# A decoder layer on one core: another queue order for the last two gated units, and three means in a row

## The chip, the cores and the metric

The kernel runs on one core of a Trainium2 chip. TensorE (PE) multiplies matrices into PSUM banks; PEld is its loading of weights. VectorE (DVE), ScalarE (ACT) and GpSimd (POOL) work beside it, each with an instruction row of its own; the SyncE queue (SP) issues nearly all DMAs. Engines wait for one another by semaphores only. The metric is the device time of one execution in microseconds (us), the median of several. TensorE's clock has two levels, 2.4 and 1.2 GHz; the profile shows which one was granted, 1.00 being the higher.

## The reference, cut to what matters

One layer of a decoder (DEPTH is 1) over 1024 prompt rows and 8 sample rows, 1032 columns in all. In the first half a combined projection feeds two groups of heads:

```
proj = x @ w_in            # q, f, i, g: 4 heads x 128 (HGRN2), u: 32 groups x 16 (S5)
f = lb + (1 - lb) * sigmoid(fz); k = (1 - lb) * sigmoid(-fz)
o_A: S_t = diag(f_t) S_{t-1} + k_t v_t^T, o_t = S_t^T q_t       # per head
o_A = o_A * rsqrt(mean(o_A^2) + eps) * norm_g * sigmoid(g)      # per head
o_B = gelu(C h + D u); o_B = o_B * sigmoid(o_B @ w_glu)         # S5
x = LayerNorm(alpha * x + concat(o_A, o_B) @ w_out)
x = LayerNorm(alpha * x + ConvFFN(x))
```

The means over 128 channels of the squares of a head's output, the sigmoid of g and the glu product with its sigmoid are what the change moves. ConvFFN is the second half and isn't touched.

## The kernel before

Data lies transposed: channels on the 128 partitions, the 1032 columns in the free dimension, in three blocks of 344. Products are made in three passes from high and low halves (wh and XH hold rounded values, wl and XL what is left), so every weight and activation that TensorE uses is first split: the high half by a copy on ScalarE, the low half by a subtraction on VectorE.

The first half is a list of steps, written by `order()` and walked by every engine. Each engine emits its own part of a step, so the list sets the order of instructions on all of them:

- `part n i` is product i of unit n on TensorE: one block of 128 rows, 3 passes x 3 column blocks, 9 matmuls of 344 columns. Units 0 to 3 are u, 4 to 15 are f, q, g of heads 0 to 3 (so 14 is q and 15 is g of head 3, the two of `DIRECT`, which stay on the chip), 16 to 19 the glu product, 20 and 21 the first two blocks of the out projection. Even units use slot 0 of weights and banks, odd ones slot 1.
- `unit n` follows the last product of a unit: ScalarE evacuates its banks (a sigmoid for 15 to 19) and makes the high half of the weights of unit n + 2.
- `lo n` is the low half of the weights of unit n on VectorE. `with_splits` puts it in: it becomes due at `unit n-2` and is written behind the second following step of the kinds part, level, values, kt, kv, o.
- `level h l` (0 to 7) is the within-chunk work of head h. TensorE does small matmuls into one of two banks, VectorE reads the bank and extends QK, from level 6 on ScalarE copies. TensorE's level l needs VectorE's step of level l - 1.
- `kt`, `kv`, `o`: transposed keys, chunk states, and the output products of a head. With `o` ScalarE copies the output and squares it. `ms h b` is the mean of block b: a matmul with a matrix of 1/128 on TensorE, Ln and Exp on ScalarE. `fin h b` multiplies output, factor and gate on VectorE. `hp_sig` and `hp_a` prepare a head.
- `gelu`, `gl`: high and low halves of the gelu rows. `z m`, `zh m`, `zl m`: glu gate row m on VectorE, its high half on ScalarE, its low half on VectorE.

Steps that are not products stand in tables, `S5_SLOTS`, `SLOTS` (one row for each head, one string for each level) and `TAIL`. A digit in a string takes as many products from a queue. The queue is filled with units in their order and, at two points, with parts of units. `put` holds the last product of unit 14 back until `("o", 1)` is in the list, and that of unit 15 until `("fin", 1, 2)` is. In a row of `SLOTS` a head's own levels stand with the `kt` to `fin` steps of the head before.

`level`, `kt`, `kv`, `o`, `ms` share two banks in turn; `bank_uses` numbers them in the order of the list. TensorE waits until the last use of the bank has been read. Ln and Exp lie in one table of ScalarE, the sigmoid in another; a table is loaded (L1060, L1133, L1163) wherever the kind changes.

Of the kernel before, what the change touches and what calls it, by code (L numbers as in the profile page):

```python
# [23 lines left out]
KD = D // P  # L24
# [59 lines left out]
DIRECT = (14, 15)  # L84


def rows_of(n):

    if n < GLU_N:
        return list(range(KD))  # L90
    if n < OUT_N:
        return list(range(HEADS))
    return list(range(HEADS, KD)) + list(range(HEADS))
# [21 lines left out]
]  # L115
TAIL = "kt 1 kv 2 o save rload wh2 wl2 2 ms0 1 ms1 1 f30 m30 ms2 1 f31 l30 m31 f32 ahead p30 l31 m32 wh3 l32 p31 p32"

def order():


    o, queue = [], []

    def unit(n, parts=None):

        last = len(rows_of(n)) - 1
        return [(1.32, [("part", n, i)] + ([("unit", n)] if i == last else []) +
                 ([(Z_AFTER[i], n - 1 - GLU_N)] if GLU_N < n < OUT_N and i in Z_AFTER else []))
                for i in (range(last + 1) if parts is None else parts)]
# [92 lines left out]
    o.append(("wv", 0))  # L221
    for n in (2, 3, *range(F_N, DIRECT[0])):
        queue += unit(n)
    queue += unit(14, range(4)) + unit(15, range(4)) + unit(14, range(4, KD)) + unit(15, range(4, KD))
    values = iter([NC, *range(NC)])
    for c in range(HEADS):
        for step, slot in zip(S5_STEPS, S5_SLOTS[c]):
# [42 lines left out]


ORDER = order()


# [2639 lines left out]
```

## Time and profile before

| | us |
|---|---|
| median of 3 runs | 1202.02 (1201.29 to 1203.36) |
| the profiled execution | 1200.96 |
| its span, first to last instruction | 1199.2 |
| TensorE busy | 1169.8 (98%) |
| VectorE busy | 814.6 (68%) |
| ScalarE busy | 507.8 (42%) |
| GpSimd busy | 181.1 (15%) |

The mean granted clock of TensorE is 0.997. Lines as L1657 are those of the kernel: L1657 is `part`, L1646 and L1676 the out projection, L1805 to L1827 the levels, L1836 `kt`, L1843 `kv`, L1854, L1855 and L1860 `o`, L1866 `ms`; on VectorE L2389 extends QK, L2423 is `kv`, L2437 and L2443 are `fin`, L2450 is `lo`, L2516 and L2517 are `z`, L2218 makes low halves; on ScalarE L1201 to L1206 are `o`, L1215 and L1217 `ms`, L1126 and L1133 units, L1068 high halves of weights, L1141 `zh`, L1222 `gelu`. The stretch that the change touches lies between 292 and 400 us.

The page has busy time of each engine, a strip of 40 slices, the DMA queues, the chain of work that ended last, and groups of instructions. A timeline lists instructions in order of time with the idle time before them in brackets and what ended it. "issue" is time in which the engine waited for nothing that the profile shows.

### The profile page before, as it was taken

What the parts mean: (1) busy time and instruction counts of PE and PEld (TensorE: products, weight loads), DVE (VectorE), ACT (ScalarE), POOL (GpSimd) and SP (SyncE); (2) the same over time, 40 slices, a digit from 0 to 9 for tenths busy, and PEclk for the clock granted to TensorE, in tenths of its full rate; (3) what the DMA queues carried; (4) which work ended last, traced back from release to release, by engine and by line L of the source; (5) the groups of instructions that cost most, each with busy time, mean ns of one, the idle gap of its engine ahead of it and who ended that gap; (6) DMA issues with size and microseconds to landing.
All of it is one profiled execution on the core that took longest, in us unless ns stands there. A gap on an engine that the chain in (4) does not pass through costs nothing.

```text
span 1199.2 us, 24092 instructions
## 1 busy us (share of the span) xinstructions
PE 1169.8 (98%) x9718; PEld 1129.0 (94%) x9718; DVE 814.6 (68%) x1498; ACT 507.8 (42%) x850; POOL 181.1 (15%) x152
## 2 busy tenths in 40 slices
PE   9999999999898999999999999999999999999996
PEld 8988889998788999999999999999999999999995
DVE  6995767557887557798627863686458844786547
ACT  5411212337756446665314541354125521554335
POOL 5210000100000244200210021001200030001365
PEclk9999999999999999999999999999999999999999
DMA  8441223518435410411372227222631255112503
GB/s 301 117 119 50 89 78 122 179 58 220 123 105 183 178 36 37 142 37 46 89 258 90 55 64 273 98 65 55 227 146 55 56 181 191 55 56 60 206 25 119
DMA packets 84815, 139.31 MB, mean 116 GB/s; under 512 B 26360, under 2 KB 52504, under 8 KB 84696
## 3 DMA queue, kind: packets, MB, share of 16 engines
q1 hardware_dynamic: 84704, 137.77, 35.9%
q8 instruction: 78, 1.28, 0.4%
q14 instruction: 33, 0.27, 0.1%
HBM read 97.89 MB, written 40.03 MB: 115 GB/s over the span
## 4 chain that ended last, share of the span: by engine, by line
PE 84%; DVE 10%; ACT 2%; issue 2%; DMA 1%; POOL 0%; SPq 0%; POOLq 0%; ACTq 0%; DVEq 0%
PE psum L1973 32%; PE psum L1945 15%; PE psum L1657 13%; PE psum L1676 6%; PE psum L2056 5%; PE psum L1734 4%; PE psum L1646 1%; DMA st<-in_xT 1%; DVE R L2583 1%; PE psum L1787 1%; PE psum L1769 1%; DVE wl L2631 1%; PE psum L1782 1%; PE psum L1854 1%; PE psum L1816 1%
## 5 line engine op out<-in xcount | busy, mean ns | idle before, releaser
L1973 PE MATMUL psum<-XH,wh 128*128 128x258 f32 x640 | 181.3, 283 | 1.7 <-ACT ub L1324 1.4
L1973 PE MATMUL psum<-XH,wl 128*128 128x258 f32 x640 | 181.0, 283 | 0.0
L1973 PE MATMUL psum<-TR,wh 128*128 128x258 f32 x640 | 181.0, 283 | 0.0
L1973 PE MATMUL psum<-XL,wh 128*128 128x258 f32 x640 | 180.0, 282 | 0.0
L1587 POOL TENSOR_TENSOR wl<-raw,wh 128x512 fp32r<-128x512 f32 (+2 forms) x36 | 57.8, 1610 | 567.8 <-ACT wh L1273 557.1
L1945 PE MATMUL psum<-AH,wl 128*128 128x344 f32 x384 | 123.1, 321 | 0.0
L1973 PEld LDWEIGHTS psum<-XH,wh 128*128 128x128 f32 x640 | 121.0, 189 | 2.2 <-issue 2.2
L1945 PE MATMUL psum<-AL,wh 128*128 128x344 f32 x384 | 123.1, 320 | 0.0
L1945 PE MATMUL psum<-AH,wh 128*128 128x344 f32 x384 | 122.9, 320 | 0.0
L1973 PEld LDWEIGHTS psum<-XL,wh 128*128 128x128 f32 x640 | 121.5, 190 | 0.1
L1973 PEld LDWEIGHTS psum<-XH,wl 128*128 128x128 f32 x640 | 120.9, 189 | 0.0
L1973 PEld LDWEIGHTS psum<-TR,wh 128*128 128x128 f32 x640 | 120.9, 189 | 0.0
L1657 PE MATMUL psum<-XH,wh 128*128 128x344 f32 x477 | 110.3, 340 | 2.0 <-DVE wl L2450 1.1
L1324 ACT ACTIVATE ub<-psum 128x258 f32<-128x258 f32 x160 | 58.8, 380 | 109.1 <-DVE hb L2649 60.1
L1657 PE MATMUL psum<-XL,wh 128*128 128x344 f32 x477 | 101.6, 321 | 0.8 <-DVE XL L2218 0.8
L1657 PE MATMUL psum<-XH,wl 128*128 128x344 f32 x477 | 101.3, 321 | 0.0
L1273 ACT ACTIVATE wh<-WS 128x512 fp32r<-128x512 f32 x80 | 50.5, 631 | 114.2 <-DVE WS L2624 114.1
L1273 ACT ACTIVATE wh<-raw 128x512 fp32r<-128x512 f32 (+2 forms) x96 | 61.2, 639 | 86.5 <-PE psum L1945 44.9
L1973 PE MATMUL psum<-TH,wh 128*128 128x258 f32 x320 | 90.8, 284 | 1.8 <-DVE wl L2631 1.5
L1973 PE MATMUL psum<-TH,wl 128*128 128x258 f32 x320 | 90.2, 282 | 0.0
L1657 PEld LDWEIGHTS psum<-XH,wh 128*128 128x128 f32 x477 | 78.1, 190 | 9.6 <-issue 3.8
L1657 PEld LDWEIGHTS psum<-XL,wh 128*128 128x128 f32 x477 | 80.7, 189 | 1.4 <-DVE XL L2218 1.4
(413 smaller groups left out, 2807.5 us busy)
## 6 DMA issues: line engine op xcount, KB each, us to landing
raw<-in_w_up SPq DMA_DIRECT2D x44, 512.0 KB, 4.1
ub<-rscr SPq DMA_DIRECT2D x16, 516.0 KB, 5.0
rscr<-ub SPq DMA_DIRECT2D x16, 516.0 KB, 3.2
raw<-in_w_dn SPq DMA_DIRECT2D x32, 256.0 KB, 3.3
raw<-in_w_units SPq DMA_DIRECT2D x15, 512.0 KB, 4.5
fscr<-st SPq DMA_DIRECT2D x10, 516.0 KB, 2.9
R<-in_xT SPq DMA_DIRECT2D x8, 516.0 KB, 6.7
RS<-rscr SPq DMA_DIRECT2D x8, 516.0 KB, 4.4
```

Of the source, the lines that this page charges most:

```text
L1273: act.activation(dst, src, ACT.Copy).then_inc(w_hi, 1)
L1324: act.activation(ubq(s, b), psum[:, bank, 0:QW], ACT.Copy).then_inc(piece, 1)
L1587: pool.tensor_tensor(dst, src, high.bitcast(F32), ALU.subtract).then_inc(w_lo, 1)
L1646: ins = nc.tensor.matmul(psum[:, 3 * slot + b, 0:CW], w, x[:, k, blk(b)], start=(first and p_ == 0), stop=(last and p_ == 2))
L1657: ins = nc.tensor.matmul(psum[:, 3 * slot + b, 0:CW], w, x[:, k, CW * b:CW * b + CW], start=(first and p_ == 0), stop=(last and p_ == 2))
L1676: last = nc.tensor.matmul(psum[:, out_bank(i), 0:CW], w, x[:, k, blk(b)], start=(k == AHEAD[0] and p_ == 0), stop=(k == HEADS - 1 and p_ = ...
L1734: last = nc.tensor.matmul(u.ps, x[:, k, cols], w[:, k, :], start=(k == 0 and p_ == 0), stop=(k == KD - 1 and p_ == 2))
L1769: last = nc.tensor.matmul(u.ps[SS * gi:SS * gi + SS, rr * UC:(rr + 1) * UC], BT[i][:, r, SS * gi:SS * gi + SS], U[:, 2 * r + gi, :], start ...
L1782: nc.tensor.matmul(o[n][e], TM[:, g, :], U[:, g, 0:NS + NL], start=(n == 0), stop=False, skip_group_check=True)
L1945: ins = nc.tensor.matmul(psum[:, bank, 0:CW], a[:, k * P:(k + 1) * P], x, start=(start and p_ == 0), stop=(stop and p_ == 2), skip_group_c ...
L1973: ins = nc.tensor.matmul(psum[:, bank, 0:QW], a[:, k * P:(k + 1) * P], x, start=(start and p_ == 0), stop=(stop and p_ == 2), skip_group_c ...
L2056: last = nc.tensor.matmul(psum[:, bank, 0:CW], w, gated(x, k)[:, blk(b)], start=(k == 0 and p_ == 0), stop=(k == nk - 1 and p_ == 2))
```

## The change

```diff
@@ -111,7 +111,7 @@  (SLOTS, the row of head 3)
-    ("1 kt 1", "1 kv 1 mld0", "2 o save", "1 ms0 1 ms1 f0", "1 s0 1 ms2 mld1 f1 f2", "2 z out 2 zh 1 zl mld2 wload", "1 mix0 1 mix1", "1 ml0 vb ml1 mix2 1 ml2"),
+    ("1 kt 1", "1 kv 1 mld0", "2 o save", "1 ms0 ms1 ms2 1 f0", "1 s0 1 mld1 f1 f2", "2 z out 2 zh 1 zl mld2 wload", "1 mix0 1 mix1", "1 ml0 vb ml1 mix2 1 ml2"),
@@ -221,7 +221,9 @@  (order)
     for n in (2, 3, *range(F_N, DIRECT[0])):
         queue += unit(n)
-    queue += unit(14, range(4)) + unit(15, range(4)) + unit(14, range(4, KD)) + unit(15, range(4, KD))
+    for parts in (range(4), range(4, KD - 1), [KD - 1]):
+        for n in DIRECT:
+            queue += unit(n, parts)
```

The queue held products 0 to 3 of unit 14, 0 to 3 of 15, 4 to 7 of 14, 4 to 7 of 15. Now it holds 0 to 3 of 14, 0 to 3 of 15, 4 to 6 of 14, 4 to 6 of 15, then 7 of 14 and 7 of 15. Since 4 to 6 of unit 15 stand ahead of product 7 of unit 14, which is held back, two of them come out earlier; from there on the steps between the products stand elsewhere relative to them. No instruction is added or taken away. Line numbers of the kernel after the change are 2 higher.

TensorE, from head 1's transposed keys (`kt`, L1836) to the first of its output products (L1854). Before:

```order
L1810 MATMUL psum<-DP0,ones_rms 32x128 x4
L1657 MATMUL psum<-XH,wh0 128x344 x3
L1657 MATMUL psum<-XL,wh0 128x344 x3
L1657 MATMUL psum<-XH,wl0 128x344 x3
L1843 MATMUL psum<-V,KTQ 128x128 x8
L1816 MATMUL psum<-QK0 30x16 x32
L1854 MATMUL psum<-SC1,V 128x128
L1855 MATMUL psum<-QK1,S_all 128x128
L1854 MATMUL psum<-SC1,V 128x128
```

Now:

```order
L1812 MATMUL psum<-DP0,ones_rms 32x128 x4
L1659 MATMUL psum<-XH,wh0 128x344 x3
L1659 MATMUL psum<-XL,wh0 128x344 x3
L1659 MATMUL psum<-XH,wl0 128x344 x3
L1845 MATMUL psum<-V,KTQ 128x128 x8
L1659 MATMUL psum<-XH,wh1 128x344 x3
L1659 MATMUL psum<-XL,wh1 128x344 x3
L1659 MATMUL psum<-XH,wl1 128x344 x3
L1818 MATMUL psum<-QK0 30x16 x32
L1659 MATMUL psum<-XH,wh1 128x344 x3
L1659 MATMUL psum<-XL,wh1 128x344 x3
L1659 MATMUL psum<-XH,wl1 128x344 x3
```

Two products of unit 15 (wh1) stand ahead of and behind level 2 of head 2 (QK0, 30x16).

VectorE, from level 4 of head 2 on. The low half of weights of unit 16 is `wl0<-raw0,wh0`. Before:

```order
L2389 TENSOR_TENSOR QK0<-QK0,DP0 128x2x64x8
L2409 COPY_PREDICATED DG<-masks,psum 128x16x8
L2382 TENSOR_TENSOR DP0<-DP0 128x64
L2450 TENSOR_TENSOR wl0<-raw0,wh0 128x512
L2218 TENSOR_TENSOR XL<-st2,XH 128x1024
L2218 TENSOR_TENSOR XL<-st2,XH 128x8
L2218 TENSOR_TENSOR XL<-ybuf,XH 128x1024
L2218 TENSOR_TENSOR XL<-ybuf,XH 128x8
L2389 TENSOR_TENSOR QK0<-QK0,DP0 128x2x32x16
```

Now, from the three steps of head 1's output to the next low half:

```order
L2439 TENSOR_TENSOR O<-O,KTQ 128x344
L2445 SCALAR_TENSOR_TENSOR O<-O,ng,SG1 128x344
L2439 TENSOR_TENSOR O<-O,KTQ 128x344
L2445 SCALAR_TENSOR_TENSOR O<-O,ng,SG1 128x344
L2439 TENSOR_TENSOR O<-O,KTQ 128x344
L2445 SCALAR_TENSOR_TENSOR O<-O,ng,SG1 128x344
L2452 TENSOR_TENSOR wl0<-raw0,wh0 128x512
L2391 TENSOR_TENSOR QK0<-QK0,DP0 128x2x16x32
L2384 TENSOR_TENSOR DP0<-DP0 128x16
L2452 TENSOR_TENSOR wl1<-raw1,wh1 128x512
```

That low half left the place behind level 4 (DP0, 128x64) and stands behind the six instructions of head 1's output, ahead of level 6 (128x2x16x32).

ScalarE, from the end of head 2's output (`O`) on; KTQ takes the squares, Ln and Exp of the means, st<-psum is the sigmoid of unit 18. Before:

```order
L1203 ACTIVATE O<-psum 128x8
L1206 ACTIVATE KTQ<-O 128x344 x3
L1060 ACT_TABLE_LOAD
L1141 ACTIVATE XH<-st 128x1032
L1215 ACTIVATE KTQ<-psum,eps_rms 128x344
L1217 ACTIVATE KTQ<-KTQ 128x344
L1133 ACT_TABLE_LOAD
L1133 ACTIVATE st<-psum 128x1032
L1068 ACTIVATE wh<-raw 128x1024
L1060 ACT_TABLE_LOAD
L1215 ACTIVATE KTQ<-psum,eps_rms 128x344
L1217 ACTIVATE KTQ<-KTQ 128x344
```

Now, one copy earlier in the row:

```order
L1203 ACTIVATE O<-psum 128x512 x2
L1205 ACTIVATE O<-psum 128x8
L1208 ACTIVATE KTQ<-O 128x344 x3
L1062 ACT_TABLE_LOAD
L1135 ACT_TABLE_LOAD
L1135 ACTIVATE st<-psum 128x1032
L1070 ACTIVATE wh<-raw 128x1024
L1062 ACT_TABLE_LOAD
L1217 ACTIVATE KTQ<-psum,eps_rms 128x344
L1219 ACTIVATE KTQ<-KTQ 128x344
L1217 ACTIVATE KTQ<-psum,eps_rms 128x344
L1219 ACTIVATE KTQ<-KTQ 128x344
```

The high half of gate row 1 (XH<-st) moved ahead of the copies, the sigmoid of unit 18 moved ahead of the first mean, and the three means follow each other. The number of table loads is the same.

On SyncE's queue one load of glu weights (raw1<-in_w_glu) moved behind the two loads for head 3. GpSimd's row is unchanged.

## Rows read from the trace of the kernel before

**Rows 1.** The page, the chain that ended last by engine.

```profile
PE 84%; DVE 10%; ACT 2%; issue 2%; DMA 1%; POOL 0%; SPq 0%; POOLq 0%; ACTq 0%; DVEq 0%
```

**Rows 2.** Timeline of TensorE: start us, us, engine, line, instruction, [idle before <-releaser].

```profile
299.55 0.72 PE L1816 MATMUL psum<-QK 128*30 128x16 f32 x64 [0.95 <-DVE S_all L2423]
301.14 0.46 PE L1854 MATMUL psum<-SC,V 128*128 128x128 f32 x2 [0.88 <-DVE S_all L2423]
...
317.13 0.23 PE L1816 MATMUL psum<-QK 128*16 128x16 f32 x7 [3.21 <-issue]
...
361.42 0.82 PE L1866 MATMUL psum<-KTQ,ones_rms 128*128 128x344 f32 x2 [1.64 <-ACT KTQ L1215]
...
372.61 0.74 PE L1657 MATMUL psum<-XH,wh 128*128 128x344 f32 x3 [1.15 <-DVE wl L2450]
```

**Rows 3.** Windows: busy us of PE, PEld, DVE, ACT, POOL; granted clock; DMA share; GB/s.

```profile
318.00:320.00 2.00, 2.00 (x9) 2.00 (x8) 2.00 (x3) 1.97 (x7) 0.00 (x0) 0.50 0.04 8
```

**Rows 4.** Chain that ended last, in order of time: start us, us, what.

```profile
308.27 1.41 PE psum L1657 x9
...
310.90 1.60 PE psum L1657 x9
...
317.36 5.99 PE psum L1657 x27
323.35 0.65 PE psum L1823 x32
...
349.60 1.70 PE psum L1860 x16
```

**Rows 5.** Timeline of ScalarE, 310 to 320 us.

```profile
310.42 1.01 ACT L1126 ACTIVATE Q<-psum 128x1032 f32<-128x1032 f32 x1
311.33 0.62 ACT L1068 ACTIVATE wh<-raw 128x512 fp32r<-128x512 f32 x1
...
319.81 0.49 ACT L1217 ACTIVATE KTQ<-KTQ 128x344 f32<-128x344 f32 x1
```

**Rows 6.** Timeline of VectorE, 312 to 325 us.

```profile
312.93 0.69 DVE L2450 TENSOR_TENSOR wl<-raw,wh 128x512 fp32r<-128x512 f32 x1
315.00 2.09 DVE L2218 TENSOR_TENSOR XL<-st,XH 128x1024 fp32r<-128x1024 f32 x2 [1.38 <-ACT XH L1223]
...
323.40 0.58 DVE L2443 SCALAR_TENSOR_TENSOR O<-O,ng,SG 128x344 f32<-128x344 f32 x1
324.02 1.22 DVE L2389 TENSOR_TENSOR QK<-QK,DP 128x1024 f32<-128x1024 f32 x1
```

**Rows 7.** Windows over two longer stretches, columns as in rows 3.

```profile
324.00:349.00 25.00, 23.82 (x295) 22.38 (x296) 23.33 (x39) 11.01 (x18) 0.00 (x0) 1.00 0.35 99
380.00:490.00 110.00, 109.17 (x693) 105.74 (x691) 68.12 (x126) 55.46 (x100) 40.10 (x35) 1.00 0.25 90
```

**Rows 8.** Timeline of ScalarE, 352 to 359 us.

```profile
352.80 1.28 ACT L1060 ACT_TABLE_LOAD   x1
354.10 1.07 ACT L1141 ACTIVATE XH<-st 128x1032 fp32r<-128x1032 f32 x1
355.07 0.53 ACT L1215 ACTIVATE KTQ<-psum,eps_rms 128x344 f32<-128x344 f32 x1
...
357.43 1.04 ACT L1133 ACTIVATE st<-psum 128x1032 f32<-128x1032 f32 x1
358.37 1.05 ACT L1068 ACTIVATE wh<-raw 128x1024 fp32r<-128x1024 f32 x1
```

**Rows 9.** Timeline of VectorE, 349 to 369 us.

```profile
349.10 0.16 DVE L2517 TENSOR_TENSOR st<-st 128x8 f32<-128x8 f32 x1
...
357.46 1.22 DVE L2389 TENSOR_TENSOR QK<-QK,DP 128x1024 f32<-128x1024 f32 x1
...
365.13 0.52 DVE L2437 TENSOR_TENSOR O<-O,KTQ 128x344 f32<-128x344 f32 x1 [1.35 <-ACT KTQ L1217]
```

**Rows 10.** Timeline of SyncE's queue: the moved load.

```profile
307.78 1.29 SPq L782 DMA_DIRECT2D raw<-in_w_glu  x1
```

## The prediction

> **What bounds the kernel now.** I read the chain of work that ended last first. It is 84% TensorE [rows 1]: nearly all that can be won or lost is a wait of TensorE, or a stretch of its lower clock. So the next view is the timeline of TensorE with its idle times, in the stretch that the change touches (292 to 400 us). It has seven waits of 0.88 us or more; five stand in [rows 2]: 0.95 and 0.88 us for VectorE's state update, 3.21 us in the middle of level 5 of head 2 where nothing that the profile shows is waited for, 1.64 us before the third mean of head 2, and 1.15 us for a split of weights. The table by windows shows what follows the 3.21 us: the granted clock is 0.50 at 318 to 320 us [rows 3], the lower of the two levels, 1.2 GHz. The three products from 317.36 take 5.99 us in place of some 4.4 (1.60 for one behind small matmuls, 1.41 for each of the others by the products at 310.90 and 308.27) [rows 4]; about 1.6 to 1.7 us is what that low stretch took.
>
> Then I ask who really sets the pace, since a wait of TensorE that is filled gains nothing where another engine is the bound. VectorE is busy 23.33 of the 25 us from 324 to 349 [rows 7]. Its level 6 runs at 324.02, right behind the three steps of head 1's output (the last instruction begins at 323.40 and takes 0.58 us), though TensorE is at level 6 only at 323.35 [rows 4, 6]. So between 315 and 350 us TensorE and VectorE are level; what is filled on TensorE is mostly lost again, and what is put into VectorE's row ahead of something TensorE needs is paid in full. From 380 to 490 us TensorE works 109.17 of 110 us [rows 7]: nothing gives a delay back after that.
>
> **The change part by part.** No instruction is added or removed. Units 14 and 15 give two of their products to the place before and after level 2 of head 2, and unit 14 now ends behind level 4, and all that is queued behind moves.
>
> *Two products earlier.* They fill the waits of 0.95 and 0.88 us [rows 2], at 1.60 us each [rows 4]: head 1's output products, and ScalarE which follows them, come 3.2 - 1.8 = 1.4 us later. Unit 14's evacuation (1.01 us) and the split of the glu weights behind it (0.62, the two overlap by 0.1) go behind the two copies of the gelu rows [rows 5], which thereby win 1.4 to 1.5 us: for VectorE the low halves of those rows stay where they are (315.00). Its split of the glu weights at 312.93 goes away there, but VectorE waited 1.38 us for ScalarE right behind it [rows 6], so nothing is won.
>
> *That split (lo 16) is the first term.* It stands now behind the three output steps of head 1, and the last of these ends at 323.98 [rows 6]. ScalarE's last factor for them was done at 320.30 (319.81 and 0.49) and is 1.4 later [rows 5], which still fits. So lo 16 runs 323.98 to 324.6. The first product of unit 16 needs it, and level 6 now stands behind that product on TensorE. Level 6 is ready at 324.6 + 1.6 + 0.65 = 326.9, and VectorE's step on it, before at 324.02, starts at 326.9: **+2.9 us**. Queued behind on VectorE are the factors of head 3, the states, level 7 and all glu gates, in the busy window of [rows 7]. Bounds: 1.2 (the 1.67 us in which VectorE is idle in that window absorb their whole sum) and 3.3.
>
> *The clock behind it.* The product at 310.90 ends at 312.5, and the mean behind it takes 0.8 as in [rows 2]; so TensorE is done with unit 15 at about 313.3 + 1.4 + 0.65 + 1.6 = 317 and waits until 324.6, or from about 320 if the stop of 3.21 us stays. Both waits are longer than 3.21 us, behind which the clock fell. The two steps on the path run in the first microseconds behind the wait. **+1.7 us**, as measured above; bounds 0 (no fall) and 3.4 (a low stretch twice as long). The old fall cost nothing that VectorE did not cost as well.
>
> *Head 2's output.* The high half of gate row 1 on ScalarE (1.07 us, [rows 8]) goes ahead of the copies of head 2's output. It waits for the gate on VectorE, which ended at 349.26 (349.10 and 0.16, [rows 9]). The copy that frees the bank for the last piece (before at 349.60, [rows 4]) takes 0.60 more; it could be 1.3 us late. The gate's place to the products comes 0.3 to 0.5 us earlier. **+0.8 us**, bounds 0 and 1.3.
>
> *The three means in a row, and unit 18's end ahead of them.* Before, behind the squares (352.80), ScalarE had a table load, a split and the first mean; unit 18's sigmoid came after it. Now the sigmoid stands first, so the table is loaded twice in a row and a third time behind it. Counted from the end of head 2's output products (349.60 + 1.70 = 351.30, [rows 4]): squares 1.5, two tables 2.56, sigmoid 0.94 (to the start of the split), split of the next weights 1.05, table 1.28, first Ln 0.53 and Exp 0.49, second Ln 0.53: 8.9 us [rows 5, 8]. The third mean waits for the first Ln (7.9), then on TensorE 0.7 for the mean, 1.6 for a product, 0.65 for level 4; VectorE starts on it at 10.8. Before it was at 357.46, which is 6.16 [rows 9]. That is 4.6 later. From there to the low half of gate row 2, which TensorE needs next, VectorE waited 1.35 us for the last factor [rows 9], which is now ready at once: 4.6 - 1.35 = **+3.2 us**. The old wait of 1.64 us for the mean [rows 2] becomes one of 4 to 4.5. Bounds: 1.5 and 4.6.
>
> *The clock again.* 4 us is more than 3.21 and more than 1.64, behind which no fall is seen. **+1.7 us**, bounds 0 and 2.3 (the two steps on the path at half speed throughout).
>
> *Transfers.* On SyncE's queue one 256 KB load of glu weights, issued at 307.78 [rows 10], moves behind the two loads for head 3, which are issued in any case. It is split into halves only behind the sigmoid of unit 15, fifteen us later: it costs nothing.
>
> Sum: 2.9 + 1.7 + 0.8 + 3.2 + 1.7 = 10.3 us. The profiled execution took 1200.96 us (span 1199.2), which gives 1211.3; it lies 1.1 under the median 1202.02, so I forecast 1202.0 + 10.3 = 1212.3.
>
> ScalarE's row shows a table load of 1.28 us with the next instruction 0.02 us behind it [rows 8], and I count that. The Trainium skill (ScalarE: Activation LUTs, What ACT_TABLE_LOAD costs) gives about 1.28 us for the load and 1.38 more for a drain at each switch of sets. By that rule the three loads ahead of the first mean would cost 4.1 us more and the sum would be 14.4, or 1216.4; no load in the stretch has such a time behind it, so the measurement decides.
>
> **Rivals.**
> - *The waits come but the clock does not fall, or falls once.* For it: I have a single fall in the stretch, and the other waits shown left the clock alone. Against it: both new waits are longer than the one that brought it. 10.3 - 3.4 = 6.9 us, 1208.9; with one fall 1210.6.
> - *The unexplained stop goes, and pays.* The 3.21 us stop sits in a burst of loads. The code ahead of it is 36 instructions longer now, so it may fall elsewhere or vanish. If TensorE were the only bound, it would win 3.2 + 1.7 = 4.9 us: 1197.1. It decides only from where VectorE's level 6 can start before 320.5; but that stands behind three output steps and two halves of gelu rows without a gap from 315.00 to 324.02, and lo 16 is added. Hardly.
> - *A worse one.* The low stretch behind the long wait lasts twice as long, or the stop comes late enough to delay level 5 as well: 2 to 4 us on top, 1214 to 1216.
> - *The delays sit in slack:* VectorE's 1.67 idle us [rows 7] and TensorE's later wait of 1.15 [rows 2] take up the first term, and the second is at its lower bound. 1.2 + 1.5 and no fall: 2.7 us, 1204.7; no measurable change if a little less.
>
> **How the numbers follow.** The forecast, both waits with both falls, 55%; no or one fall 23%; worse 10%; slack 7%; the stop pays 5%. 0.2% is 2.4 us, about what these runs can tell from no change. Faster by more: 4%, from the stop alone. Within 0.2%: 5%, part of slack and the rest of the stop. Slower: 91%. The range is 1206.0 to 1216.0: it leaves out the stop and most of the slack below, and holds the worse case to its end.
>
> **What would show it.** On TensorE a wait of 4 to 8 us before the first product of unit 16, released by VectorE's split of the weights, and one of 4 to 4.5 us before the third mean of head 2, released by ScalarE's Ln; the granted clock at 0.5 behind each; three table loads between the squares and the first mean; VectorE's level 6 near 327 and its level 4 of head 3 near 366. TensorE is otherwise unchanged from the out projection on, only later. I am wrong if the first wait is under 2 us, if lo 16 is not what ends it, or if the delay at 400 us is under 5 us.

## The result and the profile after

| | before | after |
|---|---|---|
| median of 6 runs each, us | 1202.22 (1201.06 to 1204.18) | 1211.37 (1210.86 to 1212.55) |
| ratio | 1 | 1.0075, 95% interval 1.0065 to 1.0085 |
| profiled execution / its span, us | 1200.96 / 1199.2 | 1211.24 / 1209.5 |
| granted clock, mean | 0.997 | 0.992 |
| PE busy, us | 1169.8 | 1172.9 |

The change makes the kernel 9.2 us slower by the medians and 10.3 us by the two profiled executions. Line numbers of the changed kernel are 2 higher. TensorE works as many instructions; the chain that ended last has less of it and more of the other engines than in [rows 1]:

```profile
PE 82%; DVE 11%; ACT 3%; issue 2%; SPq 1%; DMA 1%; POOL 0%; POOLq 0%; ACTq 0%; DVEq 0%
```

The timeline of TensorE, against [rows 2] (the last column in brackets is the idle time before, and who ended it):

```profile
313.95 0.70 PE L1818 MATMUL psum<-QK 128*16 128x16 f32 x64
...
324.36 1.23 PE L1659 MATMUL psum<-XH,wh 128*128 128x344 f32 x3 [8.11 <-DVE wl L2452]
...
354.84 1.92 PE L1862 MATMUL psum<-Q,S 128*128 128x1 f32 x16 [0.78 <-ACT O L1203]
...
364.83 1.40 PE L1868 MATMUL psum<-KTQ,ones_rms 128*128 128x344 f32 x2 [3.03 <-ACT KTQ L1217]
```

The waits of 0.95 and 0.88 us are filled, and the stop of 3.21 us in level 5 is gone: 64 instructions of that level run through in one piece at 313.95. In their place stand 8.11 us before the first product of unit 16, released by VectorE's split of its weights, and 3.03 us before the third mean of head 2. Windows of TensorE alone (busy us, granted clock, DMA share, GB/s), against [rows 3]:

```profile
320.00:322.00 2.00, 0.00 (x0) 0.64 0.00 0
322.00:324.00 2.00, 0.00 (x0) 0.50 0.00 0
324.00:326.00 2.00, 1.64 (x6) 0.50 0.77 265
326.00:328.00 2.00, 2.00 (x38) 0.65 0.41 130
...
358.00:360.00 2.00, 2.00 (x8) 0.53 0.80 232
360.00:362.00 2.00, 1.81 (x4) 0.62 1.01 253
...
366.00:368.00 2.00, 2.00 (x8) 0.50 0.05 19
```

There are three stretches of 1.2 GHz where before there was one. The first begins inside the wait of 8.11 us and lasts, with the half-full windows at its ends, 6.8 us; the other two 3.4 us each.

VectorE, against [rows 6] and [rows 9]:

```profile
323.62 0.69 DVE L2452 TENSOR_TENSOR wl<-raw,wh 128x512 fp32r<-128x512 f32 x1
328.04 1.23 DVE L2391 TENSOR_TENSOR QK<-QK,DP 128x1024 f32<-128x1024 f32 x1 [3.73 <-PE psum L1825]
...
369.36 1.23 DVE L2391 TENSOR_TENSOR QK<-QK,DP 128x1024 f32<-128x1024 f32 x1 [2.99 <-PE psum L1818]
```

The split (lo 16) is the last thing before level 6 of head 2, at 323.62, behind the three output steps. Level 6 comes at 328.04 (before 324.02), level 4 of head 3 at 369.36 (before 357.46). ScalarE, against [rows 8]:

```profile
357.00 1.25 ACT L1208 ACTIVATE KTQ<-O 128x344 f32<-128x344 f32 x3
358.27 1.28 ACT L1062 ACT_TABLE_LOAD   x1
359.56 1.28 ACT L1135 ACT_TABLE_LOAD   x1
360.86 1.03 ACT L1135 ACTIVATE st<-psum 128x1032 f32<-128x1032 f32 x1
361.78 1.05 ACT L1070 ACTIVATE wh<-raw 128x1024 fp32r<-128x1024 f32 x1
362.85 1.28 ACT L1062 ACT_TABLE_LOAD   x1
364.14 0.55 ACT L1217 ACTIVATE KTQ<-psum,eps_rms 128x344 f32<-128x344 f32 x1
```

Between the squares and the first Ln stand three table loads, the sigmoid of unit 18 and a split: from 357.00 to 364.14, 7.1 us. The third mean (364.83) follows the end of that Ln. After 400 us the kernel is the old one, only later: the state's products of head 3 begin at 400.61 where they began at 390.34.

### The profile page after: what moved, and what is told of

It reads as the page before. It is cut to its first block, busy times and chain, and to the rows that moved or that the text cites. A ratio compares the mean times of both kernels' runs of the same rounds, so it can differ in the third digit from the quotient of the medians.

```text
span 1209.5 us, 24091 instructions
## 1 busy us (share of the span) xinstructions
PE 1172.9 (97%) x9718; PEld 1130.8 (93%) x9718; DVE 815.6 (67%) x1498; ACT 508.2 (42%) x850; POOL 180.7 (15%) x152
## 3 DMA queue, kind: packets, MB, share of 16 engines
q8 instruction: 78, 1.28, 0.4%
## 4 chain that ended last, share of the span: by engine, by line
PE 82%; DVE 11%; ACT 3%; issue 2%; SPq 1%; DMA 1%; POOL 0%; POOLq 0%; ACTq 0%; DVEq 0%
PE psum L1975 31%; PE psum L1947 15%; PE psum L1659 12%; PE psum L1678 6%; PE psum L2058 5%; PE psum L1736 4%; PE psum L1648 1%; DVE QK L2391 1%; DVE R L2585 1%; PE psum L1789 1%; PE psum L1771 1%; DVE wl L2633 1%; PE psum L1784 1%; PE psum L1862 1%; DVE TR L2590 1%
```

## The experiments

Each kernel ran beside the kernel before on the same chip. For the finer comparisons I count from one point that all traces share, VectorE's step on level 2 of head 2 (about 301 us), to three later ones; in the kernel before these are 23.0 us (level 6 of head 2), 56.4 us (level 4 of head 3) and 89.3 us (the state's products of head 3, behind which all kernels run alike). The table shows how much later each one is there. It leaves out what happened ahead of the changed stretch.

| kernel | median, us | against before | level 6 | level 4 | end |
|---|---|---|---|---|---|
| after | 1211.37 | +9.2 | +4.0 | +11.9 | +10.3 |
| q: queue order alone | 1210.06 | +8.1 | +4.3 | +9.1 | +8.6 |
| s: means in a row alone | 1202.48 | +0.5 | +1.8 | +2.8 | +2.2 |
| row1: unit 14's last row one place back | 1208.01 | +5.9 | -0.1 | +5.6 | +5.1 |
| a_early: after, lo 16 ahead of the output steps | 1209.92 | +7.9 | +2.5 | +10.3 | +8.7 |
| unit18: after, unit 18's end behind the means | 1206.92 | +4.6 | +4.3 | +6.2 | +5.7 |
| ulo: both of these | 1207.06 | +4.7 | +1.2 | +3.8 | +3.1 |
| zh1: after, gate row 1 behind the copies | 1213.04 | +10.9 | +4.3 | +13.4 | +11.7 |
| warm1: after, first wait filled | 1210.66 | +8.7 | +2.7 | +10.9 | +9.3 |
| warm2: and 19 products at the mean | 1217.68 | +15.3 | +2.7 | +13.1 | +11.5 |
| shift: before, instructions shifted | 1207.28 | +5.2 | +0.2 | +1.5 | +1.5 |
| better: before, five steps moved | 1201.14 | -1.2 | +1.3 | +2.0 | +0.4 |
| better_s: and instructions shifted | 1201.23 | -0.9 | +1.2 | 0.0 | -1.7 |

### The two halves of the change

q takes the new queue order alone:

```diff
-    queue += unit(14, range(4)) + unit(15, range(4)) + unit(14, range(4, KD)) + unit(15, range(4, KD))
+    for parts in (range(4), range(4, KD - 1), [KD - 1]):
+        for n in DIRECT:
+            queue += unit(n, parts)
```

> The kernel before with the new queue order of units 14 and 15 alone; the means of head 2 keep their old places in the order (ms0, a row, ms1, ..., ms2). Unit 18 still stands whole ahead of the first mean, because the queue shifted it there. Theory 1 (the queue order carries nearly all of it; the means in a row add only the last few tenths and a second fall of the clock): +7.5 to +8.5 us against before, a wait of 8 us before the first product of unit 16, released by VectorE's split of its weights, TensorE at half clock behind it, two table loads fewer than three waits in a row, no stop of 3.2 us at 314. Theory 2 (my forecast's terms taken apart: split behind the output steps 2.9, clock 1.7, gate row 0.8; the means in a row carry the other 3.2 + 1.7): +5.4 us.

s takes the row of SLOTS alone:

```diff
-    ("1 kt 1", "1 kv 1 mld0", "2 o save", "1 ms0 1 ms1 f0", "1 s0 1 ms2 mld1 f1 f2", "2 z out 2 zh 1 zl mld2 wload", "1 mix0 1 mix1", "1 ml0 vb ml1 mix2 1 ml2"),
+    ("1 kt 1", "1 kv 1 mld0", "2 o save", "1 ms0 ms1 ms2 1 f0", "1 s0 1 mld1 f1 f2", "2 z out 2 zh 1 zl mld2 wload", "1 mix0 1 mix1", "1 ml0 vb ml1 mix2 1 ml2"),
```

> The kernel before with the means of head 2 in a row alone (the queue as before, so unit 18's last row stands behind the three means). Theory 1: the wait for the third mean is covered by less work, but the second and third table loads of before go (all three means come before a sigmoid): +0.3 to +0.8 us, clock 1.00 there, the stop of 3.2 us at 314 still there. Theory 2 (the means in a row carry term D by themselves): +3.2 us, or +4.9 with a fall of the clock.

q took 1210.06 us (ratio 1.0071, 1.0057 to 1.0085), s 1202.48 (1.0003, 0.9995 to 1.0012). The queue order alone carries 8.1 of the 9.2 us, and the means in a row alone nothing that can be measured. Behind the new queue order the means may carry the rest, 1.1 us by the medians and 1.7 by the traces; the intervals of q and of the changed kernel overlap. In q the 8.11 us stand before unit 16, and the wait behind the means has only another name: it now comes before level 4, which follows the second mean there.

```profile
324.52 1.23 PE L1659 MATMUL psum<-XH,wh 128*128 128x344 f32 x3 [8.11 <-DVE wl L2452]
...
365.30 0.72 PE L1818 MATMUL psum<-QK 128*24 128x16 f32 x64 [3.24 <-ACT KTQ L1217]
```

The sigmoid of unit 18 ahead of the first mean is the queue's doing as well. The function `put` holds unit 14's last row back until the output step of head 1 is in the order, and as long as this row heads the queue, the places in front stay empty; those are the two waits of 0.9 us in [rows 2]. With rows of unit 15 in front of it the places are filled, and every row behind comes earlier in the order, unit 18's last one too. The three means in a row add little to that.

### How much comes with one row

row1 puts unit 14's last row behind one row of unit 15's second half; the changed kernel puts it behind three.

```diff
-    queue += unit(14, range(4)) + unit(15, range(4)) + unit(14, range(4, KD)) + unit(15, range(4, KD))
+    queue += unit(14, range(4)) + unit(15, range(4)) + unit(14, range(4, KD - 1)) + unit(15, range(4, 5)) + unit(14, [KD - 1]) + unit(15, range(5, KD))
```

> The kernel before with unit 14's last row behind the first row of unit 15's second half, where the changed kernel has it behind all three of them: a third of the queue change, and nothing else. Theory 1 (what the new queue order costs is that unit 14 ends later, with the copy of its result, which frees the bank and the weights for unit 16; each row it is put back moves the chain of unit 16 by part of 1.42 us until VectorE's output steps stand ahead of the split): between +3 and +5.5 us against before, with a wait of 2 to 4 us before unit 16. Theory 2 (the cost is all in the order of VectorE's queue behind it, which flips only with the last of the three rows): within 1 us of before.

It took 1208.01 us (1.0048, 1.0034 to 1.0061), a little over the range of the first theory, but not for the reason expected; the second theory, within 1 us of before, missed too. There is no wait before unit 16, and level 6 of head 2 is where it was. The stop in level 5 is still there, and the loss comes later:

```profile
317.48 0.31 PE L1816 MATMUL psum<-QK 128*16 128x16 f32 x16 [3.28 <-issue]
...
361.94 0.70 PE L1816 MATMUL psum<-QK 128*24 128x16 f32 x64 [1.66 <-ACT KTQ L1215]
...
374.58 0.86 PE L1657 MATMUL psum<-XH,wh 128*128 128x344 f32 x3 [3.27 <-DVE XL L2218]
```

One row in front of unit 14's last fills one of the two empty places, and that is enough to bring unit 18's end ahead of the first mean: in row1's ScalarE row three table loads (355.38, 356.66, 359.95 us) and the sigmoid stand between the squares and the first Ln, as in the changed kernel. So this half of the loss does not need the other.

### The two places on VectorE and ScalarE

All four of the kernels in this section take the changed kernel and move steps in the finished order. a_early:

```diff
-    return with_splits(o)
+    return early_lo(with_splits(o))
+
+
+def early_lo(o):
+
+    o.remove(("lo", 16))
+    i = o.index(("level", 2, 5))
+    return o[:i + 1] + [("lo", 16)] + o[i + 1:]
```

> The changed kernel with VectorE's split of unit 16 moved up from behind the three output steps of head 1 (and gate row 1's last product) to right behind level 5 of head 2. Theory 1 (the split's place behind the output steps, term A of 2.9 us, sets the wait before unit 16): that wait shrinks from 8.1 to about 5 us (it is then released by the split or by ScalarE's copy of unit 14, with the output steps now later for nothing), and 2.3 to 2.9 us of the 9.2 come back: +6.3 to +7 against before. Theory 2 (something else releases unit 16, or the output steps delayed by 0.6 us pass it on to level 6): less than 1 us comes back.

unit18, with the helper of the next two kernels (`behind(x, y)` takes step x out and puts it right behind y):

```diff
+    behind(("unit", 18), ("ms", 2, 2))
+    behind(("zl", 1), ("unit", 18))
```

> The changed kernel with ScalarE's copies and sigmoid of unit 18 (and the split behind them) moved from ahead of the three means of head 2 to behind them; TensorE's order is the same. Theory 1 (what ends TensorE's wait for the third mean is ScalarE's work ahead of it: the sigmoid with two table loads more): two table loads of 1.28 and the copies go from the path, the wait of 3.0 us before the third mean goes, level 4 and the output steps of head 2 come earlier; 3.5 to 4.5 us of the change's 9.2 come back: +4.7 to +5.7 against before. Theory 2 (the third mean waits for the squares, which follow the output copies, wherever the sigmoid stands): less than 1 us comes back.

ulo has `behind(("lo", 16), ("level", 2, 5))` in front of these two lines.

> Both single moves together in the changed kernel: VectorE's split of unit 16 ahead of head 1's output steps, and unit 18's copies and sigmoid behind the three means. Theory 1 (the two places are separate terms and add up, 2.3 to 2.9 and 3.5 to 4.5): +2.5 to +3.5 us against before remain, which is the wait of 4.9 us before unit 16 that neither removes. Theory 2 (one term hides the other): +4.5 or more.

unit18 took 1206.92 us (1.0047, 1.0034 to 1.0060): 4.5 us of the loss come back, about as expected (3.5 to 4.5). In its ScalarE row the first Ln now follows the squares with one table load between, and the wait before the third mean is gone:

```profile
357.57 1.25 ACT L1219 ACTIVATE KTQ<-O 128x344 f32<-128x344 f32 x3
358.84 1.28 ACT L1073 ACT_TABLE_LOAD   x1
360.23 0.55 ACT L1228 ACTIVATE KTQ<-psum,eps_rms 128x344 f32<-128x344 f32 x1
```

a_early took 1209.92 us (1.0064, 1.0050 to 1.0078), 1.5 us less than the changed kernel where 2.3 to 2.9 were expected. Its wait before unit 16 did shrink as expected, from 8.11 to 4.87 us, but it started later: TensorE's clock had fallen once more, ahead of it, with hardly a wait there.

```profile
308.00:310.00 2.00, 1.86 (x70) 0.90 0.15 28
310.00:312.00 2.00, 2.00 (x8) 0.50 1.08 315
312.00:314.00 2.00, 2.00 (x69) 0.74 0.97 151
```

The same instructions run at 1.00 in the trace of the changed kernel. And what a_early wins at the end is not the split's. At level 6 it is 1.5 us ahead of the changed kernel; another low stretch follows at 340 us, and the third mean comes 63.8 us behind the common point in both. From there to level 4 it takes 2.93 us, in the changed kernel 4.53 (364.83 to 369.36), with the same instructions between, because the clock stayed at 1.00 behind this wait:

```profile
365.54 0.82 PE L1875 MATMUL psum<-KTQ,ones_rms 128*128 128x344 f32 x2 [3.28 <-ACT KTQ L1224]
...
368.47 1.23 DVE L2398 TENSOR_TENSOR QK<-QK,DP 128x1024 f32<-128x1024 f32 x1 [1.40 <-PE psum L1825]
```

These 1.6 us are there at the end as well (+8.7 against +10.3). ulo against unit18 is the cleaner pair, since neither trace has such a fall ahead of level 6: the split's place is worth 3.1 us at level 6 and 2.5 at the end. By the medians that pair shows nothing (1207.06 and 1206.92): ulo's eight runs lie between 1204.18 and 1211.22, at mean clocks from 0.995 to 0.990. Its median, +4.7, is what the second theory foresaw (one term hides the other); only its trace (+3.1) fits the first. So the 2.5 us rest on the traces and on the 1204.2 and 1204.3 us of ulo's two best runs, not on its ratio (1.0038, 1.0023 to 1.0052). What is left ahead of level 6 in ulo is a wait of 4.97 us before unit 16:

```profile
320.59 0.69 DVE L2464 TENSOR_TENSOR wl<-raw,wh 128x512 fp32r<-128x512 f32 x1
...
321.34 1.23 PE L1671 MATMUL psum<-XH,wh 128*128 128x344 f32 x3 [4.97 <-DVE wl L2464]
```

There level 5 and two low halves of gelu rows stand ahead of the split on VectorE. This wait is 1.2 of ulo's 3.1 us. The other 1.9 arise behind level 6. From level 7 of head 2 to level 2 of head 3 VectorE takes 15.1 us in place of 14.0: the low half of unit 18's weights (0.69 us) stands ahead of that level 2 in the new order, behind it in the old. From level 2 to level 3 it takes 8.6 in place of 7.5, with gate row 1's copy ahead of head 2's output on ScalarE. Level 4 adds 0.4, and 0.6 come back behind it. The changed kernel has the same two steps of 1.1; no run moves unit 18's low half alone.

zh1 has the single line `behind(("zh", 1), ("s0_load", 3))`.

> The changed kernel with ScalarE's high half of gate row 1 moved from ahead of head 2's output copies to behind them. Theory 1 (the copy of 1.0 us in front of the output copies is no separate cost: the wait of 0.8 us before the state's products of head 2 goes and is added to the wait before the third mean, because ScalarE's chain behind it is as long as before): the changed kernel's time within 0.5 us. Theory 2 (my forecast's term for it): 0.8 us less.

It took 1213.04 us (1.0092, 1.0078 to 1.0105), 1.7 more than the changed kernel: both expectations missed the time. The wait of 0.78 us is gone, but the low clock behind unit 16's wait lasted longer than in the changed kernel, up to 330.5 us in place of 327.4:

```profile
326.00:328.00 2.00, 2.00 (x26) 0.50 0.48 152
328.00:330.00 2.00, 2.00 (x25) 0.50 0.00 0
330.00:332.00 2.00, 2.00 (x13) 0.87 0.24 14
```

The order ahead of 350 us is the same in both, so this is not the move's doing. What the move did can be counted from VectorE's step on level 7 of head 2, behind that low stretch:

```profile
335.02 1.23 DVE L2401 TENSOR_TENSOR QK<-QK,DP 128x1024 f32<-128x1024 f32 x1 [0.66 <-PE psum L1839]
...
366.18 1.49 PE L1878 MATMUL psum<-KTQ,ones_rms 128*128 128x344 f32 x2 [5.72 <-ACT KTQ L1227]
```

The third mean comes 31.2 us behind it; in the changed kernel 31.1 (333.74 to 364.83). The squares come 1.0 us earlier, and the copy of 1.06 us now stands between them and the first Ln. So its place costs nothing at the third mean, which is the mechanism of the first theory. The loss against the changed kernel lies in the clock: 1.1 us up to level 7, and 0.4 from the third mean to level 4, around which the low clock lasted 6.8 us in place of 3.4; together the 1.5 us that the traces differ by at the end. All four runs of zh1 had a mean clock of 0.990 to 0.992 (changed kernel: 0.991 to 0.994). Why it stayed low for longer there isn't known.

### The clock

warm1 fills the wait before unit 16 with products of constants that nothing reads:

```diff
+                    if (c, i) == (16, 0):
+                        pe.wait_ge(evac[s], c // 2)
+                        for _ in range(24):
+                            nc.tensor.matmul(psum[:, 3 * s, 0:P], ones_rms[:, :], ones_ln[:, :], start=True, stop=True)
```

> The changed kernel with 24 added float32 products of constants, 128x128, some 6.2 us in all by the 0.26 us of one in the opening row of such products, into unit 16's bank while TensorE would wait for its split: no data or wait of the work changes. Theory 1 (the idle time before unit 16 drops the clock to half for 6.8 us behind it, which costs 3.4 us of TensorE's products, of which some is taken up by the waits behind it): clock 1.00 at 320 to 328, the stretch behind the wait runs at the pace of the kernel before, and 1.5 to 3 us come back. Theory 2 (the low clock lies beside the waits for VectorE and costs nothing): the clock stays high and the time is the changed kernel's within 0.3 us. If the products are longer than the wait they cost their excess.

It took 1210.66 us (1.0074, 1.0062 to 1.0086). The clock stays at full speed there until 361 us. Unit 16 starts where it did (324.71 us, of which 0.33 is from ahead of 301), and level 6 is 1.3 us earlier than in the changed kernel:

```profile
318.07 5.62 PE L1697 MATMUL psum<-ones_ln,ones_rms 128*128 128x128 f32 x48 [1.48 <-ACT Q L1128]
324.71 0.75 PE L1659 MATMUL psum<-XH,wh 128*128 128x344 f32 x3 [1.02 <-DVE wl L2456]
...
363.87 1.49 PE L1872 MATMUL psum<-KTQ,ones_rms 128*128 128x344 f32 x2 [4.66 <-ACT KTQ L1217]
```

At the end 0.9 us of it is left in the trace, 0.7 in the medians: less than the 1.5 to 3 of the first theory, more than the 0.3 of the second. The second part of what it shows: without a fall at 358 the wait before the third mean is 4.66 us long, in the changed kernel 3.03 behind a fall. The fall at 358 cost nothing, for ScalarE set the time of the third mean. The 1.3 us of level 6 are still there at the third mean (62.5 us behind the common point, in the changed kernel 63.8). Around the longer wait the low clock then lasted 6.8 us in place of 3.4, from 361 to 368, and took 0.3 of them back.

warm2 was to fill that wait as well:

```diff
-                    pe.wait_ge(sq_ready, NB * c + step[2] + 1)
                     b = step[2]
                     u = Use(step)
+                    if (c, b) == (2, 2):
+                        for _ in range(19):
+                            nc.tensor.matmul(u.ps[:, 0:P], ones_rms[:, :], ones_ln[:, :], start=True, stop=True)
+                    pe.wait_ge(sq_ready, NB * c + b + 1)
```

> The kernel with 24 added products in the wait before unit 16, and 19 more of them (4.4 us by 0.234 us of one in that kernel) in the wait of 4.66 us before the third mean of head 2, into the bank of that mean. Theory 1 (the clock falls are the effect of the idle stretches, and the second one's cost now reaches the end): clock 1.00 from 316 to 370, and 1 to 2 us less than with the first 24 alone, so +6.5 to +7.5 against before. Theory 2 (what is won is waited for again by the next step that VectorE or ScalarE releases): within 0.5 us of the kernel with 24 alone.

This one failed as a test and taught something else. The added products waited too, and came behind the wait, on the path:

```profile
363.97 4.51 PE L1873 MATMUL psum<-ones_ln,ones_rms 128*128 128x128 f32 x38 [3.20 <-ACT KTQ L1217]
368.32 0.74 PE L1875 MATMUL psum<-KTQ,ones_rms 128*128 128x344 f32 x2
```

`Use` is the wait for the bank. So the third mean waits for its bank, which the Ln of the first mean sets free, and not for its squares. The profiled execution took 1213.05 us, the other three 1217 to 1219 at lower clocks; without traces of them, why they are 4 us longer stays open.

### The stop, and a better order

shift puts 32 tiny products in the place of one of the ten opening ones:

```diff
-            for i in range(WARM):
+            for i in range(WARM - 1):
                 nc.tensor.matmul(psum[:, 5, 0:P], ones_rms[:, :], ones_ln[:, :], start=True, stop=True)
+            for i in range(32):
+                nc.tensor.matmul(psum[0:16, 5, 0:16], ones_rms[:, 0:16], ones_ln[:, 0:16], start=True, stop=True)
```

> The kernel before with one of the ten opening products of constants replaced by 32 tiny ones (16x16), which cost the same 0.5 to 0.7 us in all but put 124 more instructions into TensorE's stream (weights and products), so that every block of 16 KB of instructions is fetched 124 instructions earlier in the program. Theory 1 (the stop of 3.2 us before level 6 of head 2 is a block of instructions whose fetch fell late into the transfers of 308 to 316): the stop goes, and the wait for VectorE that it hid comes in its place: 0 to 2.5 us less than before. Theory 2 (the stop is something else): it stays at the same instruction, and the time is before's within 0.5 us. Rival of my forecast: the stop goes and is paid back in full, -3.2 us or more.

The DMA view points to the cause of the stop. In the kernel before, no block of instructions moved from 305 to 314.6 us; one came in the next 2.4 us (packets, MB, share):

```profile
q1 hardware_dynamic: 175, 0.62, 64.2%
q8 instruction: 1, 0.02, 2.4%
```

In the changed kernel a block moved before 312 us:

```profile
q1 hardware_dynamic: 1516, 0.77, 44.5%
q8 instruction: 1, 0.02, 0.8%
```

The other traces with the stop agree: in s, row1 and better no block moved in the 9 us ahead of it, and one moved while TensorE stood. In shift, too, the stop at level 5 is gone and a wait for VectorE stands in its place, with a fall of the clock behind it:

```profile
324.06 0.83 PE L1825 MATMUL psum<-QK 128*32 128x32 f32 x32 [2.28 <-DVE QK L2391]
```

Level 6 is as late as with the stop (+0.2): the stop cost nothing that VectorE would not have cost. But new stops of 0.76 and 1.28 us came at 231 and 282 us, and shift took 1207.28 us (1.0037, 1.0025 to 1.0050), against both theories and against the rival. Its loss lies ahead of the stretch: its common point comes at 304.40 us, 3.4 later than before, and only 1.5 are added behind it.

```profile
231.34 0.24 PE L1818 MATMUL psum<-QK 128*28 128x16 f32 x5 [0.76 <-issue]
...
282.61 0.37 PE L1818 MATMUL psum<-QK 128*16 128x16 f32 x28 [1.28 <-issue]
```

better moves five steps in the order of before:

```diff
+    behind(("part", 18, 1), ("level", 3, 3))
+    behind(("part", 18, 2), ("ms", 2, 0))
+    behind(("vb", 2), ("kt", 2))
+    behind(("lo", 17), ("hp_a", 3, 0))
+    behind(("s0_scale", 3), ("unit", 19))
```

> The kernel before (old queue order, means in their old places) with five single steps moved where a wait of its trace ends: two products of unit 18 later (one behind level 3 of head 3, one behind the first mean of head 2, as cover), the keys' scaling vb of head 2 behind the step kt, split 17 behind the first part of head 3's decays, and ScalarE's scaling of head 3's state behind unit 19. Theory 1 (TensorE waits at these places for the engine's order alone, 1.4 + 0.7 + 0.7 + 0.7 by a replay of the measured durations): 2 to 3.5 us less than before. Theory 2 (each is taken up by the next wait, or the clock falls at another place): within 1 us of before.

better_s is that order with the opening products of shift.

> The kernel with five single steps moved from before's order (the one that took 1201.1 us), with the same tiny products at the start, so that its stop of 3.8 us and the 7 us of half clock behind it should go as well. Theory 1: 1.5 to 4 us less than before, the stop gone, a wait of 2 to 3 us for VectorE before level 6 of head 2 in its place. Theory 2 (the stop hides a wait as long as itself): the same as that kernel without them, about -1.2 us.

They took 1201.14 us (0.9993, 0.9985 to 1.0002) and 1201.23 us (0.9991, 0.9982 to 1.0000): by the medians 1.2 and 0.9 us less than before. So the second theory of each holds, and the gains of 2 to 3.5 and 1.5 to 4 us that the first ones named did not come. From the common point on the trace of better_s is 1.7 us shorter than that of before, and it has no wait at the means. Both beat the changed kernel by 10 us; neither is clearly faster than the kernel before, since both intervals reach 1.0000.

## Why the prediction was right, step by step

The forecast was 1212.3 us in 1206.0 to 1216.0; measured 1211.37. The mechanism was right: the two waits came where they were foreseen, ended by what was foreseen, with the low clock behind each. Most sizes are close. That the sum fits to a tenth of a microsecond is luck, as the terms below show.

- **lo 16 behind the output steps, 2.9, and the clock behind it, 1.7.** Both were foreseen for level 6: +4.6, measured +4.0. The clock alone was 1.3 by warm1, so the wait itself carries 2.7. The wait was foreseen at 7.6 us, from 317 to 324.6; it was 8.11, from 316.25 to 324.36. It began earlier because the two products put TensorE back by 0.9 us (the first mean of head 1 at 308.35, before 307.43), where 1.4 had been foreseen. Level 6 came at 328.04; the sign "near 327" left the low clock out.
- **But the step named as its cause is only part of it.** With the split ahead of the output steps the wait is still 4.9 us, and level 6 is 1.2 us late in ulo: two low halves of gelu rows and level 5 stand ahead of the split as well. The forecast counted from where the split stood, and did not ask how far up it would have to go to cost nothing.
- **Head 2's output, 0.8.** The wait for ScalarE's copy is there (0.78 us). VectorE's step from level 2 to level 3 of head 3 takes 1.1 us longer with it. But zh1 took the wait away, and the third mean came no earlier: ScalarE has the copy in its row either way, and where it leads, the term is worth nothing.
- **A term that was missing.** The low half of unit 18's weights stands ahead of level 2 of head 3 on VectorE, where it stood behind. The step from level 7 to level 2 takes 1.1 us longer in the changed kernel, and so it does in q, row1, unit18, ulo, zh1 and warm1. On the other side 0.8 of the +4.0 were gone by level 7. The forecast had neither.
- **Unit 18's end ahead of the means, 3.2, and the second fall, 1.7.** Together 4.9; unit18 gives back 4.5 by medians and 4.6 in the traces. The fall alone is 1.6 (the changed kernel against a_early from the third mean on), so about 3 are left for the order. Three table loads stand where they were foreseen. But the forecast put it under "the three means in a row", and that edit alone costs 0.5 us by the medians (interval -0.6 to 1.4); it is the queue that brings unit 18 forward, as row1 shows with one row.
- **The waits as signs.** 4 to 4.5 us before the third mean was foreseen, 3.03 seen: the clock had fallen 7 us earlier, at 358, so TensorE came later to the same point. Without that fall it is 4.66 (warm1). The stretch at 358 is one that no term had, and it cost nothing.
- **Level 4 of head 3 "near 366".** That sign was written without the two falls. The terms give 2.9 + 1.7 + 0.8 + 4.6 + 1.7 = 11.7 there, and 11.9 was measured; from there 1.6 us came back where 1.35 had been foreseen.
- **The stop.** "The stop goes, and pays" was given 5%. It went, and paid nothing: shift shows the wait for VectorE that it had covered.
- **The sum.** 10.3 forecast, and 10.28 measured between the two profiled executions. Up to level 6 the forecast had 4.6 for 4.0; behind it 5.7 for 6.3, with a term missing, 0.8 given back at level 7 and 0.8 counted for a copy that the third mean never felt. These errors cancelled. The medians differ by only 9.2. The profiled execution of before had a mean clock of 0.997, as 8 of its 50 later runs had (median 1201.6 us); 32 of them had 0.995 (1202.2), six 0.993 (1203.7). So its ordinary run has a little more low clock than the trace that the sum started from. I read the rest of the difference as that, but no run separates it.

Three table loads of 1.28 us stand at 358.27, 359.56 and 362.85 with the next instruction 0.01 to 0.02 us behind each. The Trainium skill (ScalarE: Activation LUTs, What ACT_TABLE_LOAD costs) gives a drain of about 1.38 us more at each switch of sets. By an estimate from that figure the third mean would have come 4.1 us later than it did; this trace does not agree. The kernel before has three loads between its squares and its third mean too (352.80, 356.14, 359.43), so even by that rule the 4.1 us would not all have been the change's.

## What to carry to other kernels

When rows are moved in a queue, look at what the shift brings forward or back on the other engines before looking at the rows themselves: here one row that filled an empty place brought the rows behind it forward, and with them a sigmoid, with two more table loads, ahead of a mean that TensorE needed. Filling a wait of 0.9 us on TensorE wins nothing if what TensorE needs next stands behind more work in another engine's row for it. Add a sum from one trace to that trace's own time, and see from the clocks of the other runs how ordinary that trace is.

## What the runs showed of the hardware

- **The clock can fall with hardly a wait ahead of it, and not in every run.** In a_early it fell at 309.6 us with TensorE idle for only 0.14 of the 2 us around it, and in s at 302 behind 0.88 us of idle time. The traces of the changed kernel (309) and of before (302) run the same instructions at 1.00. Ahead of 309.6, and of the fall at 358 in the changed kernel, TensorE had worked on products of one column and the small ones of a level. The windows of s:

```profile
302.00:304.00 2.00, 2.00 (x12) 0.52 0.12 33
304.00:306.00 2.00, 2.00 (x14) 0.62 0.03 8
```

- **Most of the spread of one kernel's runs goes with its clock.** The 50 later runs of the kernel before lie between 1200.97 and 1204.25 us: the six at a mean clock of 0.993 all at 1203.0 or more, the eleven at 0.996 or 0.997 all under 1202.5.
- **A block of instructions can come late.** One block fetched in the busy DMA stretch of 308 to 316 us stopped TensorE for 3.2 to 3.8 us (before, s, row1, better), always in level 5 of head 2. 124 added instructions took it away there and made two shorter stops elsewhere.
- **Low clock is cheap where another engine leads.** The changed kernel spends 13.7 us at 1.2 GHz in the stretch, by its windows, against 3.4 before. Some 3.8 of them lie in the wait of 8.11 us, where nothing runs, and TensorE's busy time is 3.1 us longer than before. The first stretch cost 1.3 us at level 6 (warm1), the second, at 358, nothing, since ScalarE led.
- **Where TensorE leads, it is paid in full.** The third stretch, behind the third mean, cost 1.6 us from there to level 4 (4.53 us, in a_early 2.93 at 1.00), and the 1.6 us were still there at the end.
